# SyncE loads latent and rotary pages one by one by page numbers in registers; POOL keeps the K and V gathers; prompt keys are projected two heads at a time

## What is computed

```python
# latent attention of the samples; past_len 4096, PAGE_SIZE 128, 8 heads
def paged_rows(pool):
    return pool[page_table].reshape((B, past_len) + pool.shape[2:])
ckv_all = concatenate([paged_rows(pool_ckv), c_kv], axis=1)      # rows of 256
kpe_all = concatenate([paged_rows(pool_kpe), k_pe], axis=1)      # rows of 32
s = einsum('bqhc,bkc->bhqk', q_lat, ckv_all) + einsum('bqhr,bkr->bhqk', q_pe, kpe_all)
p = softmax(where(k_pos <= q_pos, s * 96 ** -0.5, -1e30))
o = einsum('bqhc,chv->bqhv', einsum('bhqk,bkc->bqhc', p, ckv_all), w_uv)
# sparse attention of the samples: the 256 best of the 4104 keys of each of 64 queries
idx = indexer_topk(q_i, w_i, pos, ik_all, 256)
k_sel, v_sel = gather_selected(pool_k, ...idx...), gather_selected(pool_v, ...idx...)   # rows of 512
# prompt: keys by head, k[h] = c_kv @ w_uk[:, h], 64 wide, 8 heads
```

## Time and profile before

| | |
|---|---|
| median of 3 runs | 1749.62 us (1746.54 to 1753.55) |
| the profiled execution | 1741.32 us, of which the span of its instructions is 1739.5 us |
| busy share of the span | PE 93%, DVE 50%, ACT 24%, POOL 19% |
| mean granted TensorE clock | 0.963 of full speed |

### The profile page before, as it was taken

How to read it: one execution, slowest core, us unless ns; L and a number is a source line. 1 busy time by engine, 2 the same in 40 slices (tenths; PEclk the granted TensorE clock), 3 DMA queues, 4 the chain that set the end, 5 groups by cost and what they waited for, 6 DMA issues and landing times.

```text
span 1739.5 us, 21664 instructions
## 1 busy us (share of the span) xinstructions
PE 1626.2 (93%) x8572; PEld 999.0 (57%) x8572; DVE 866.3 (50%) x1636; ACT 421.6 (24%) x1111; POOL 337.0 (19%) x348
## 2 busy tenths in 40 slices
PE   6999989999999898998687899999999999989998
PEld 3554444446776666665454566547777777744443
DVE  3448798998522887874877742222322323210011
ACT  2131312001015545644355531001111111100010
POOL 2000000010004777770555630000000000000000
PEclk9899989999999999998798899999999999999999
DMA  8311212142306788877555845302122122111100
GB/s 247 141 62 61 106 42 98 63 167 86 135 36 242 264 283 298 278 264 219 144 147 150 280 134 182 115 20 89 49 73 73 49 73 73 49 61 49 65 23 32
DMA packets 89846, 218.38 MB, mean 126 GB/s; under 512 B 13576, under 2 KB 37520, under 8 KB 83696
## 3 DMA queue, kind: packets, MB, share of 16 engines
q0 software_dynamic: 29168, 116.66, 20.2%
q1 hardware_dynamic: 59506, 93.24, 16.2%
q10 hardware_dynamic: 1072, 7.09, 1.4%
HBM read 199.99 MB, written 16.84 MB: 125 GB/s over the span
## 4 chain that ended last, share of the span: by engine, by line
PE 77%; DVE 9%; POOL 6%; issue 3%; DMA 3%; ACT 2%; ACTq 0%; SPq 0%; DVEq 0%
PE PS L630 13%; PE PS L2063 13%; PE PS L2108 11%; PE PS L2091 7%; PE PS L681 7%; POOL mem L1820 5%; PE PS L2040 4%; PE PS L1538 2%; PE PS L746 2%; PE PS L2017 2%; DVE mem L1732 2%; PE PS L1408 2%; DVE mem L1731 1%; PE PS L1051 1%; PE PS L2471 1%
## 5 line engine op out<-in xcount | busy, mean ns | idle before, releaser
L630 PE MATMUL PS<-mem 128*128 128x512 f32 (+3 forms) x580 | 234.8, 561 | 0.0
L2063 PE MATMUL PS<-mem 128*128 128x376 f32 x704 | 231.7, 481 | 0.0
L2108 PE MATMUL PS<-mem 128*128 128x512 f32 (+1 forms) x440 | 192.2, 599 | 1.4 <-DVE mem L2287 1.4
L2063 PEld LDWEIGHTS PS<-mem 128*128 128x128 f32 x704 | 131.0, 189 | 79.3
L630 PEld LDWEIGHTS PS<-mem 128*128 128x128 f32 (+1 forms) x580 | 100.5, 186 | 119.8 <-issue 119.5
L1820 POOL DMA_INDIRECT mem<-in_cache_dsa_k,mem x128 | 143.9, 1124 | 43.6 <-issue 38.4
L1820 POOL DMA_INDIRECT mem<-in_cache_dsa_v,mem x128 | 122.5, 957 | 145.4 <-PE PS L1520 113.1
L2108 PEld LDWEIGHTS PS<-mem 128*128 128x128 f32 (+1 forms) x440 | 80.7, 184 | 112.3 <-issue 110.7
L2091 PE MATMUL PS<-mem 128*128 128x216 f32 x704 | 135.8, 345 | 0.0
L2091 PEld LDWEIGHTS PS<-mem 128*128 128x128 f32 x704 | 129.2, 189 | 10.7
L2268 DVE TENSOR_SCALAR mem<-mem 128x528 f32<-128x528 f32 x22 | 12.2, 555 | 238.8 <-ACT mem L2171 238.8
(11 more groups left out here) (312 smaller groups left out, 2087.7 us busy)
## 6 DMA issues: line engine op xcount, KB each, us to landing
mem<-in_w_in SPq DMA_DIRECT2D x10, 2048.0 KB, 8.2
mem<-in_w_ffn_g SPq DMA_DIRECT2D x11, 1024.0 KB, 5.4
mem<-in_w_ffn_u SPq DMA_DIRECT2D x11, 1024.0 KB, 5.4
mem<-in_w_ffn_d SPq DMA_DIRECT2D x10, 1024.0 KB, 5.0
tmp_gates<-mem SPq DMA_DIRECT2D x16, 296.0 KB, 2.1
mem<-tmp_gates SPq DMA_DIRECT2D x16, 296.0 KB, 4.0
mem<-in_w_o SPq DMA_DIRECT2D x2, 2048.0 KB, 11.8
mem<-in_x_prompt SPq DMA_DIRECT2D x6, 512.0 KB, 13.6
```

Of the source, the lines that this page charges most:

```text
L630: ins = pe.matmul(PS[0:n, b[bank], out_at:out_at + width], left[:, k, cols], w[:, k, at:at + width], start=k == 0, stop=k == k_range - 1)
L2063: pe.matmul(PS[:, 3 * (f % 2) + j, 0:UP_A], w[:, k, :], h2T[:, k, 0:UP_A], start=k == 0, stop=k == KD - 1)
L2108: return pe.matmul(PS[0:TW[m], (5 * n + m) % 8, :], upT[:, f, token_cols(m)], w[:, i, :], start=f == 0, stop=f == NF - 1)
```

## The change

SP takes over the rotary and latent loads. `sp_pages` loads 8 page numbers from the page table in DRAM into SP registers, with a test that each lies in the pool; then SP issues one DMA for each page, into 16 partitions. The loads of sequence 0 are issued between the stores of gate tiles 8 to 12, those of sequences 1 to 7 behind the small loads of `sp_sample`. POOL keeps the K and V gathers. `idx_ckv` is no longer computed. The slot that lies on `vb` moves to fifth place, and the reloads of `kT` and `vb` at the stage's end change places. PE no longer waits for the gates' stores at the head of stage 2. `kn` and `kl` project two heads at a time, into 128 partitions. The transposes of input tiles 2 to 4 move behind unit qi 1. `K_FROM` goes from 4 to 1.

```diff
-        def gp_latent_load(gp, n):
...
-                gp.indirect_dma_start(kpe_raw, None, kpe_rows,
-                                      bass.IndirectOffsetOnAxis(ap=idx_row[:, b:b + 1], axis=0)).then_inc(
-                    sem("kpe_in"), tick("kpe_in", b, by=16))
+        def sp_pages(sp, b, first, n):
+            return nc.values_load_multi_w_load_instructions(
+                I["page_table"][b:b + 1, first:first + n], engines=[mybir.EngineType.SP], min_val=0,
+                max_val=I["cache_mla_ckv"].shape[1] - 1)[1]
+        def sp_kpe_load(sp, b):
+            if b:
+                sp.wait_ge(sem("sturned"), upto("sturned", ("p", b - 1, 1)))
+            for k in range(4):
+                for i, page_no in enumerate(sp_pages(sp, b, 8 * k, 8)):
+                    src = I["cache_mla_kpe"][0, bass.ds(page_no, 1)].rearrange("o (p r) d -> (o p) (r d)", p=16)
+                    sp.dma_start(kpe_raw[16 * i:16 * i + 16, 256 * k:256 * k + 256], src).then_inc(
+                        sem("kpe_in"), tick("kpe_in", *((b,) if k == 3 and i == 7 else ()), by=16))
+        def sp_latent_load(sp, n):
+            b, k = n // 4, n % 4
             if n >= 8:
-                gp.wait_ge(sem("latents_used"), upto("latents_used", n - 8))
-            gp.indirect_dma_start(raw_slot(n), None, ckv_rows,
+                sp.wait_ge(sem("latents_used"), upto("latents_used", n - 8))
+            for i, page_no in enumerate(sp_pages(sp, b, 8 * k, 8)):
+                src = I["cache_mla_ckv"][0, bass.ds(page_no, 1)].rearrange("o (p r) c -> (o p) (r c)", p=16)
+                sp.dma_start(raw_slot(n)[16 * i:16 * i + 16, :], src).then_inc(
+                    sem(f"ckv_in{n % 8}"), tick(f"ckv_in{n % 8}", *((n,) if i == 7 else ()), by=16))
@@ sp_gates, behind the store of gate tile i
+                if i == 8:
+                    sp.wait_ge(sem("heads_stored"), upto("heads_stored"))
+                    sp_kpe_load(sp, 0)
+                if 9 <= i < 13:
+                    sp_latent_load(sp, i - 9)
@@ sp_sample
             phase_a_done(sp)
+            gates_done(sp)
...
+            wait_stored(sp, "vb")
+            for b in range(1, NB):
+                sp_kpe_load(sp, b)
+                for k in range(4):
+                    sp_latent_load(sp, 4 * b + k)
@@ pe_latent
-            phase_a_done(pe)
+            pe.wait_ge(sem("turned_act"), upto("turned_act", "kb", 4, 0))
@@ POOL
-            for n, q in gather_order:
-                if q is None:
-                    gp_latent_load(gp, n)
-                else:
-                    gp_gather(gp, "k", q)
+            for q in range(NS):
+                gp_gather(gp, "k", q)
@@ kn on PE, m now counts pairs of heads
-                    ins = pe.matmul(PS[0:64, b[0], :], wuk[:, c, 64 * m:64 * m + 64], ckvT[:, c, 0:512],
+                    ins = pe.matmul(PS[:, b[0], :], wuk[:, c, 128 * m:128 * m + 128], ckvT[:, c, 0:512],
@@ start of PE
-                if i == 0:
+                if i == 1:
                     for m in range(2, NTILE):
                         turn_x(m)
```

More of the change, by code:

```diff
@@ L160, in trunk @@
         idx_row = K.take(NB, dtype=U32)
-        idx_ckv = K.take(NB, 4, dtype=U32)
+        K.take(NB * 4)
         small = K.take(64)
@@ L249, in trunk @@
         vb_at = qb_at + 2 * 4 * NCOL
-        slots = [C2.take(2048) for _ in range(4)]
-        slots[3:3] = [mem[:, vb_at:vb_at + 2048]]
+        slots = [C2.take(2048) for _ in range(4)] + [mem[:, vb_at:vb_at + 2048]]
         slots += [C.take(2048) for _ in range(3)]
@@ L318, in trunk @@
         units = [(k, m) for k in ("qi", "sm", "cq", "uq") for m in range(NTILE)]
-        units += [("wt", 0)] + [("kn", h) for h in range(H)] + [("kl", 0), ("ql", 0), ("ql", 1)]
+        units += [("wt", 0)] + [("kn", p) for p in range(H // 2)] + [("kl", 0), ("ql", 0), ("ql", 1)]
         units += [(k, m) for k in ("vm", "qb", "kb", "vb") for m in range(NTILE)]
@@ L458, in act_unit @@
             elif kind == "kn":
-                act.copy(kT[0:64, m, 0:512], PS[0:64, b[0], :]).then_inc(sem("unit_act"), tick("unit_act", *u))
+                act.copy(kT[0:64, 2 * m, 0:512], PS[0:64, b[0], :])
+                act.copy(kT[0:64, 2 * m + 1, 0:512], PS[64:128, b[0], :]).then_inc(
+                    sem("unit_act"), tick("unit_act", *u))
             elif kind == "kl":
-                act.copy(kT[0:64, :, 512:528], PS[0:64, b[0], 0:128].rearrange("p (h n) -> p h n", h=H)).then_inc(
-                    sem("unit_act"), tick("unit_act", *u))
+                for par in range(2):
+                    ins = act.copy(kT[0:64, par:H:2, 512:528],
+                                   PS[64 * par:64 * par + 64, b[0], 0:64].rearrange("p (h n) -> p h n", h=4))
+                ins.then_inc(sem("unit_act"), tick("unit_act", *u))
             elif kind == "ql":
@@ L656, in pe_unit @@
                 for c in range(2):
[L657 removed]
+                    ins = pe.matmul(PS[:, b[0], :], wuk[:, c, 128 * m:128 * m + 128], ckvT[:, c, 0:512],
                                     start=c == 0, stop=c == 1)
             elif kind == "kl":
[L660 removed]
+                for p in range(H // 2):
                     for c in range(2):
[L662 removed]
+                        ins = pe.matmul(PS[:, b[0], 16 * p:16 * p + 16], wuk[:, c, 128 * p:128 * p + 128],
                                         ckvT[:, c, LAST:LAST + 16], start=c == 0, stop=c == 1)
@@ L690, in trunk @@
         ROWS_B = 0
-        K_FROM = 4
+        K_FROM = 1
         for b in range(NB + 1):
@@ L724, in wait_stored, with gates_done @@
                 eng.wait_ge(sem(f"stored_{name}_p"), upto(f"stored_{name}_p", 4))
+        def gates_done(eng):
+            for i in range(2):
+                eng.wait_ge(sem(f"gates_stored{i}"), upto(f"gates_stored{i}", len(gate_tiles) - 2 + i))
         def phase_a_done(eng):
@@ L991, in dots @@
                         close(b - 2)
+                    if b == 0 and k == 0:
+                        wait_unit_read(pe, ("gt", len(gate_tiles) - 1))
                     if k >= 2:
@@ L2439, in _ @@
             link(dve.tensor_scalar(tb[:, 0:NB], ta[:, 0:NB], 4.0, quarter[:, 0:1], ALU.mult, ALU.add))
[L2440 to L2443, removed]
+            dve.tensor_copy(idx_row, tb[:, 0:NB]).then_inc(sem("index_ready"), tick("index_ready"))
             h_out(NTILE - 1)
```

23 lines of the change are left out of this document (3 added, 20 removed).

## The result

The changed kernel takes 2007.03 us (median of 4 runs, 2001.91 to 2012.54). The kernel before, run beside it, takes 1748.08. The ratio is 1.1479, 95% interval 1.1431 to 1.1528: slower by 259 us, on the side that was forecast, three times as far, and outside the range. The profiled execution took 2003.8 us, 1.8 above its span.

A forecast was written before the change was run, and what follows sets the result against it. POOL's queue was taken to bound the latent stage, PE close behind; after the change, SP. Profiled 1741.3 us, +88 (early part's −7 contained) and +8 for the runs' median gave 1838 us; range 1712 to 1930.

The forecast's parts named there:

- SP becomes the pacer: Latent stage: SP's eight page groups take 46 us a sequence against 32.6 before, so SP sets the pace; chance 0.53.
- g = 5.8 us: SP's time for eight pages: DMAs 2.9, 25 register steps 1.5, two register loads 1.4 us; ends 3.7 and 8.2.
- its own formula: Latent stage's end, the prompt's first product, at 576.5 + 56 g us, g being SP's time for eight pages; break-even 4.2.
- I take 0: Sequence 0's page groups among the gate stores cost nothing, hidden by buffers and banks; 5 to 10 us if g over 7.
- Early part, −7: Before the latent stage: start +2, kn −8.0, kl −1.0 us, so gate stores end at 522 in place of 529.
- The start: PE's first units: with the transposes behind qi 1, qi 2 starts at 42.2 to 44.8 us, taken as +2 us.
- POOL and the K gathers at nothing: Latent stage: 40 fewer indirect DMAs on POOL and earlier K rows were costed at nothing while SP paces.
- POOL's queue first: Latent stage before the change: POOL's 21 indirect DMAs pace it at 32.6 us a sequence, PE's work close behind.
- Narrow transfers as a rival at 1904: Latent stage: landing in 16 partitions paces, 14 us a load and 56 a sequence, +155, 1904 us; chance 0.14.
- SP keeping up, 1716: Rival for the latent stage: SP's groups stay cheap, PE becomes the bound, −33.5, 1716 us on the runs; chance 0.27.

The follow-up runs named there:

- e6: Changed kernel with each page written to 16 partitions eight apart instead of 16 neighbouring ones, page table, tests and register loads kept: 2094.4 us, ratio 1.2002.
- e1: Changed kernel with page numbers fixed when the program is built, so no register load, test or address step on SP: 1883.3 us, ratio 1.0806.
- e2: Changed kernel without the two test instructions for each page number; register loads and address steps stay: 1907.7 us, ratio 1.0948.
- e4: Changed kernel with one load of all 32 page numbers for a sequence, kept for rotary and latent loads: 1899.3 us, ratio 1.0893.
- e7: Changed kernel with sequence 0's four rotary groups one behind each of gate stores 6 to 9, latent groups one store later: 1992.9 us, ratio 1.1423.
- e11: Kernel before with the change's early parts, rotary loads of sequences 2 to 7 on SP, PE entering the stage early: 1743.5 us, ratio 0.9987.
- e10: Changed kernel with page numbers fixed when the program is built and each page spread over all 128 partitions: 1753.8 us, ratio 1.0049.
- the first experiments: e1, e2 and e4, the runs that took register work away from SP in the changed kernel: 1883.3, 1907.7 and 1899.3 us.
- e9: Kernel before with the change's early parts and rotary loads of sequences 1 to 7 on SP, without tests: 1754.5 us, ratio 1.0052.
- e12: Changed kernel with pages over 128 partitions, real table, one load of 32 numbers, no tests, sequence 0's rotary groups moved: 1792.5 us, ratio 1.0266.

## Why the prediction was right and wrong

- **SP becomes the pacer**: right, shown by e6 (a price added to its issue is paid in full) and by e1, e2 and e4 (work taken off it is gained until the next limit).
- **g = 5.8 us**: wrong, 8.45, and here most of the miss lies: 148 of 174 us. Each of the three terms was too small. "Eight DMAs: 2.9 us" and the eight address steps in the 1.5, together 3.4, are 4.0: each address is two instructions, not one. The 16 test steps "at 0.06, the gap above" were 1.0 and are 2.0: a test's larger instruction lasts 147 ns, over twice the 0.06 of the sum and five times the 28 ns of its lower end. "I take half of what that load has beyond its issue ... Two: 1.4 us" was 2.4 with the gaps: 0.9 for each, for 2 words as for 8. Steps of a kind that no row showed were priced by a gap between two issues.
- **The range**: the text had 8.2 us as its upper bound for g, which its own formula turns into 1972 us; the range was cut at 7.4, 1930. With that bound and the 10 us that the text named for the gate stores it would have reached 1982. 2007 lies outside that too, since 8.45 is above the bound: the tests had no upper price of their own. (Its other ends are loose as well: by the same formula g = 4.5 gives 1765, not 1760, and g = 7.4 gives 1927; the lower end 1712 stands for a case whose own sum is 1716.)
- **"I take 0" for sequence 0 among the gate stores**: wrong, +21 us. Four rotary groups kept SP from storing for 33 us, not 23; ScalarE waited 19.6 us for a landed store, PE 5.2, 1.8 and 1.0 behind it, and the lateness went on from tile to tile since a latent group and a store, 8.4 to 8.8 us, were longer than a tile of 8.0 and left SP no time to catch up. About 19 of the 21 are these; the rest is the early part, below. e7 returned 14 of them. The text had named the condition (g over 7), at 5 to 10 us.
- **Early part, −7**: right in sign, −5.1 at the units behind `kl` (276.85 for 281.95). The start cost 2.4, as forecast. This is not yet seen at qi 2 (41.74 for 41.46), but qi 2 then takes 9.13 us for 7.05, at a mean granted clock of 0.77 (part of it at half clock) for 1.00, right behind 10.8 us in which PE was busy for 4.4. qi 3 starts 2.4 us late, and so do the transposes ahead of kn. From its first product to that of kl, kn saved 7.0 of the forecast 8.0; kl saved 0.1 of 1.0. Now, qi 2, qi 3 and those transposes:

```profile
41.74 9.13 PE L633 MATMUL PS<-mem 128*128 128x512 f32 x16
51.14 7.05 PE L633 MATMUL PS<-mem 128*128 128x512 f32 x16
256.63 2.35 PE L2485 MATMUL PS<-mem 80*96 80x80 f32 x16 [6.04 <-DVE mem L531]
```

and before, qi 3 and the transposes:

```profile
48.78 7.05 PE L630 MATMUL PS<-mem 128*128 128x512 f32 x16
254.26 2.35 PE L2471 MATMUL PS<-mem 80*96 80x80 f32 x16 [6.02 <-DVE mem L528]
```

- **POOL and the K gathers at nothing**: right. POOL waits 265.7 us for DVE's scores in the changed kernel.
- **POOL's queue first in the stage before**: not borne out as it stands. With one of its 21 indirect DMAs gone (e11) the pace fell by 0.6 us where 1.5 were expected, and the time did not fall measurably. Which of POOL, PE and DVE holds the rest stays open.
- **Narrow transfers as a rival at 1904**: the mechanism is real. Alone, in e1, it gives 1883. That the numbers lie so close is in part luck: the sum took four loads of 14 us a sequence and no rotary load, while e1's 51.3 us hold the rotary pages too. It is not what paced the changed kernel, but it stands 16 us a sequence under it, so cheaper register work alone could never have brought back the time of before.
- **SP keeping up, 1716**: nothing came near. Even with free page numbers and 128 partitions SP needs 34.0 us a sequence (e10).

## What to carry to other kernels

Price a queue by every instruction that it gets, registers, tests and address steps too, and keep the upper bound of a price that no row shows inside the range. Before moving loads to another queue, multiply its time for one piece by the pieces in a burst: an indirect DMA of 1 MB costs POOL 1.25 us; the same megabyte in eight page DMAs costs SP 4.0, even with the page numbers at hand. And when one limit is removed, look at the next: here two lay within 25% of each other, and each hid the other in the first experiments.

## What the runs showed of the hardware that was not expected

- A load of registers costs 0.11 us a register in bulk (medians 0.89 for 8, 3.51 for 32 in e4; 4.08 for 32 in e9), and 0.9 us for the two words of a pointer. In e9, at the head of the stage, one took 4.2 us and the next 9.6. The Trainium skill, *Runtime: NRT & Kernel Launch*, § Instruction fetch mechanics, gives about 200 ns a register even in bulk; here it is about half.
- The same page to 16 partitions eight apart costs SP 0.496 us to issue, to 16 neighbours 0.316, with the register addresses of the changed kernel; a page to all 128 partitions costs 0.333 (e12).
- Halving the products of kl, each twice as wide, saved 0.1 of 2.0 us. Its rows, now and before (count, busy us, mean ns):

```profile
L665 PE MATMUL PS<-mem 128*128 128x16 f32 x16 | 1.9, 257 | 0.0
L665 PEld LDWEIGHTS PS<-mem 128*128 128x128 f32 x16 | 1.9, 192 | 0.5 <-issue 0.5
```

```profile
L662 PE MATMUL PS<-mem 128*64 128x16 f32 x32 | 2.0, 208 | 0.0
L662 PEld LDWEIGHTS PS<-mem 128*64 128x64 f32 x32 | 2.0, 138 | 0.6 <-issue 0.6
```

Products and weight loads (PEld) are busy for the same time in both, and a load of 128 columns takes 192 ns where one of 64 takes 138. So the loads seem to set the time here; no run changes them alone.
